# Router products at the two mixers' ends: weights stationary in four column tiles, in place of the token tiles

## What is computed

```python
for i in range(2):
    y = _gated_deltanet_mixer(x, ...) if i == 0 else _mla_mixer(x, ...)
    x = _layernorm(ALPHA * x + y, ln1_g[i], ln1_b[i])
    y = _grouped_moe(x, router_w, router_bias, w_gate[i], w_up[i], w_down[i])
    x = _layernorm(ALPHA * x + y, ln2_g[i], ln2_b[i])

def _grouped_moe(x, router_w, router_bias, ...):
    scores = sigmoid(x @ router_w)      # 512 x 1024 by 1024 x 16
    ...                                 # best group, top 2 in it, gates
```

## Time and profile before

| | |
|---|---|
| median of three runs | 1567.25 us (1565.63 to 1567.25) |
| time of the profiled execution | 1567.03 us |
| its span | 1565.2 us |
| DeltaNet ends, mixture 0 begins | about 905 us |
| attention ends, mixture 1 begins | about 1365 us |
| TensorE busy | 95% of the span |
| VectorE busy | 56% |

### The profile page before, as it was taken

The page is one execution under the profiler, slowest core; times in us unless marked ns, Lnnn a source line. Parts: engine busy times, 40 slices in busy tenths (PEclk is TensorE's granted clock), DMA queues, the critical chain, the costliest instruction groups (busy, mean ns, idle before and its releaser), DMA issues. The chain is left out here.

```text
span 1565.2 us, 22321 instructions
## 1 busy us (share of the span) xinstructions
PE 1479.6 (95%) x8210; PEld 917.2 (59%) x8210; DVE 871.6 (56%) x1734; ACT 349.4 (22%) x745; POOL 171.7 (11%) x196
## 2 busy tenths in 40 slices
PE   8898999999999999999999989999999999889996
PEld 5477686685775866857868643334654544543332
DVE  2785766756857667568575652216435354743117
ACT  4223222222222222212212211111332322111110
POOL 0200202002002020020010220003100000120011
PEclk9899999999999999999999989999999999799999
DMA  7751212102111121020150359997011115369983
GB/s 233 235 180 42 81 28 81 40 13 88 46 54 43 38 77 30 26 80 0 40 202 28 135 181 387 412 391 240 1 66 38 50 39 218 142 253 386 413 337 132
DMA packets 124510, 215.46 MB, mean 138 GB/s; under 512 B 11696, under 2 KB 59120, under 8 KB 124448
## 3 DMA queue, kind: packets, MB, share of 16 engines
q1 hardware_dynamic: 109984, 169.44, 30.5%
q10 hardware_dynamic: 9536, 27.27, 4.7%
q0 software_dynamic: 4928, 17.89, 3.1%
HBM read 182.92 MB, written 31.65 MB: 137 GB/s over the span
## 5 line engine op out<-in xcount | busy, mean ns | idle before, releaser
L451 PE MATMUL bank<-xT,wgu 128*128 128x512 f32 x448 | 210.4, 600 | 0.0
L1758 PE MATMUL bank<-wgu,moe_xgT 128*32 128x512 f32 x1536 | 171.4, 594 | 5.9 <-issue 2.9
L496 PE MATMUL bank<-wd,oT 128*128 128x512 f32 x256 | 118.3, 604 | 2.2 <-ACT oT L838 1.3
L451 PEld LDWEIGHTS bank<-xT,wgu 128*128 128x128 f32 x448 | 78.1, 191 | 64.3 <-issue 63.6
L537 PE MATMUL bank<-wd,xT 128*128 128x256 f32 x512 | 115.8, 379 | 0.0
L1758 PEld LDWEIGHTS bank<-wgu,moe_xgT 128*32 128x32 f32 x1536 | 50.1, 110 | 109.0 <-issue 107.3
L537 PEld LDWEIGHTS bank<-wd,xT 128*128 128x128 f32 x512 | 96.7, 190 | 12.8
L1018 DVE SCALAR_TENSOR_TENSOR wgu<-bank,taps,wgu 128x510 f32<-128x510 f32 (+1 forms) x128 | 95.2, 744 | 12.0 <-ACT wgu L733 8.1
L2005 DVE TENSOR_TENSOR moe_hid<-moe_silu,bank 128x256 f32<-128x256 f32 x24 | 10.1, 421 | 160.1 <-ACT moe_silu L1863 160.1
L1781 PE MATMUL bank<-wd,moe_hidT 128*32 128x512 f32 x768 | 87.0, 593 | 5.4 <-DVE moe_hidT L2009 3.1
L1139 DVE TENSOR_TENSOR wgu<-wgu,bank 128x512 f32<-128x512 f32 x112 | 73.9, 683 | 8.8 <-PE bank L600 3.4
(11 more groups left out here) (341 smaller groups left out, 2409.6 us busy)
## 6 DMA issues: line engine op xcount, KB each, us to landing
wgu<-moe_w_gate SPq DMA_DIRECT2D x32, 1024.0 KB, 12.8
wgu<-moe_w_up SPq DMA_DIRECT2D x32, 1024.0 KB, 14.5
wd<-moe_w_down SPq DMA_DIRECT2D x32, 1024.0 KB, 15.4
wgu<-dn_w_in SPq DMA_DIRECT2D x32, 512.0 KB, 3.8
slots_x<-gains SPq DMA_DIRECT2D x1, 9984.0 KB, 37.6
wd<-dn_w_in SPq DMA_DIRECT2D x8, 1024.0 KB, 5.3
wd<-dn_w_out ACTq DMA_DIRECT2D x16, 512.0 KB, 3.8
xT<-slots_x ACTq DMA_DIRECT2D x16, 512.0 KB, 8.3
```

What stands on the lines that cost most here:

```text
L451: mm = pe.matmul(bank[:], wqkv[:, ct, k], xT[:, k], start=k == 0, stop=k == KD - 1)
L496: mm = pe.matmul(ps[uses.at[f"{name}{n}"][0]][:], oT[:, h, tt], wo[:, h, half * 512:(half + 1) * 512], start=h == 0, stop=h == 1)
L1758: mm = pe.matmul(ps[2][seats].rearrange("p (a f) -> p a f", a=2), xgT[:, j % ROW_BUFS, k, seats], wgu[:, e % RING, :, k], start=k == 0, st ...
```

## The change

The two operands change places. `route` becomes three steps:

- `route_parts` (TensorE): for each of the eight channel pieces `k`, the router's weights are stationary and the 128 tokens of the tile move. The stationary operand is two neighbouring pieces of `route_w` side by side, 32 columns, in column tile `k % 4` of the array, so that the result stands in 32 partitions of a PSUM bank: 16 of them hold the wanted part of piece `k`, 16 hold something that isn't used. Pieces `k` and `k + 4` accumulate in the same partitions. The result is 4 x 32 partitions by 128 tokens.
- `keep` (ScalarE): the 128x128 partial sums are copied from the bank to SBUF, over the tile's piece 0 of `xT`.
- `route_sum` (TensorE): one product with that copy as the stationary operand and a new table of ones and zeros (`C_SUM`, 128x16) as the moving one adds the four partial sums of each expert and turns the result, so that the logits stand in bank 7 as before.

The partial sums of even and odd tiles use two banks in turn (2 and 3 in DeltaNet, 6 and 7 in attention, where `turn` now has two banks in place of three).

```diff
@@ -44,7 +44,8 @@
 C_SEAT = C_SIDE + 16
 CAP = 96
 C_IOTA = C_SEAT + P
-C_ALL = C_IOTA + P
+C_SUM = C_IOTA + P
+C_ALL = C_SUM + 16
 
 
 def constants():
@@ -76,6 +77,8 @@
     c[:, C_SIDE + 8:C_SIDE + 16] = eight < r % 8
     c[:, C_SEAT:C_SEAT + P] = 1.0 + np.arange(P)[None, :] % CAP
     c[:, C_IOTA:C_IOTA + P] = np.arange(P)[None, :]
+    for g in range(4):
+        c[:, C_SUM:C_SUM + 16] += r == 32 * g + 16 * (g == 3) + np.arange(16)[None, :]
     inv = (1.0 / (10000.0 ** (np.arange(0, 64, 2, dtype=np.float32) / np.float32(64)))).astype(np.float32)
     c[:, C_FREQ:C_FREQ + 32] = inv[None]
     return c
@@ -251,7 +254,7 @@
         rs_added, kq_rs_added = sem("rs_added"), sem("kq_rs_added")
         cols_in, cols_turned, weighted, weights_summed = (sem(n) for n in ("cols_in", "cols_turned", "weighted", "weights_summed"))
         weights = wba[:].rearrange("p k (j e) -> p k j e", e=NE)
-        rows = Arrival(nc, t, sb, sem, 0, summed=lambda n: (y_ready, 1 + 8 * (NK - 1) + n + 1))
+        rows = Arrival(nc, t, sb, sem, 0, summed=lambda n: (y_ready, 1 + 8 * (NK - 1) + n + 1), part_banks=(2, 3))
         zeros = t["gains"][0:CAP, 1, 1]
 
 
@@ -679,11 +682,16 @@
                             project_out(uses, "end", i, i, n, h)
                         if n in (3, 5, 7):
                             rows.turn(pe, n // 2 - 1)
+                        if n == 7:
+                            rows.route_sum(pe, 0)
                         if n in (5, 7):
-                            rows.route(pe, n // 2 - 2)
+                            rows.route_parts(pe, n // 2 - 2)
                     rows.turn(pe, TT - 1)
-                    rows.route(pe, TT - 2)
-                    rows.route(pe, TT - 1)
+                    rows.route_sum(pe, 1)
+                    for tt in (2, 3):
+                        rows.route_parts(pe, tt)
+                    for tt in (2, 3):
+                        rows.route_sum(pe, tt)
 
             pe.wait_ge(taps_kept, 1)
             pe.wait_ge(dve_sums, 1)
@@ -1306,10 +1314,12 @@
 class Arrival:
 
 
-    def __init__(self, nc, t, sb, sem, which, banks=(4, 5, 6), summed=None):
-        self.nc, self.t, self.which, self.banks, self.summed = nc, t, which, banks, summed
+    def __init__(self, nc, t, sb, sem, which, banks=(4, 5, 6), summed=None, part_banks=()):
+        self.nc, self.t, self.which, self.banks, self.summed, self.part_banks = nc, t, which, banks, summed, part_banks
         self.g, self.b = t["gains"][:, which % 2, 0], t["gains"][:, which % 2, 1]
         self.mv, self.rstd, self.neg = sb(f"row_mv{which}", [P, TT, 2]), sb(f"row_rstd{which}", [P, TT]), sb(f"row_neg{which}", [P, TT])
+        if summed:
+            self.parted, self.kept = sem(f"parted{which}"), sem(f"kept{which}")
         self.stats_ready, self.spread_ready, self.rstd_added, self.rstd_ready, self.centred, self.normed, self.turned, self.xT_ready, self.logits, self.weighed = (
             sem(f"{n}{which}") for n in ("stats_ready", "spread_ready", "rstd_added", "rstd_ready", "centred", "normed", "turned", "xT_ready_again", "logits", "weighed"))
 
@@ -1356,15 +1366,31 @@
                 mm = pe.transpose(ps[self.banks[n % of]][:, k * P:(k + 1) * P], self.t["res"][:, tt, (half * 4 + k) * P:(half * 4 + k + 1) * P], ident)
             mm.then_inc(self.turned, 1)
 
-    def route(self, pe, tt):
+    def part(self, tt):
+        return self.t["ps"][self.part_banks[tt % 2]][:, P:2 * P]
+
+    def route_parts(self, pe, tt):
         if tt == 0:
             pe.wait_ge(self.t["route_ready"], 3)
+        if tt >= 2:
+            pe.wait_ge(self.kept, tt - 1)
         for k in range(KD):
-            if k % 4 == 0:
+            n = k % 4
+            if n == 0:
                 pe.wait_ge(self.xT_ready, 2 * tt + 1 + k // 4)
-            mm = pe.matmul(self.t["ps"][7][:, tt * NE:(tt + 1) * NE], self.t["xT"][:, k, tt * P:(tt + 1) * P], self.t["route_w"][:, self.which // 2, k], start=k == 0, stop=k == KD - 1)
+            two = self.t["route_w"][:, self.which // 2, k - (n == 3):k - (n == 3) + 2].rearrange("p k e -> p (k e)")
+            mm = pe.matmul(self.part(tt)[32 * n:32 * n + 32], two, self.t["xT"][:, k, tt * P:(tt + 1) * P], start=k < 4, stop=k >= 4)
+        mm.then_inc(self.parted, 1)
+
+    def route_sum(self, pe, tt):
+        pe.wait_ge(self.kept, tt + 1 if tt < 2 else TT)
+        mm = pe.matmul(self.t["ps"][7][:, tt * NE:(tt + 1) * NE], self.t["xT"][:, 0, tt * P:(tt + 1) * P], self.t["const"][:, C_SUM:C_SUM + 16], start=True, stop=True)
         if tt == TT - 1:
             mm.then_inc(self.logits, 1)
+
+    def keep(self, act, tt):
+        act.wait_ge(self.parted, tt + 1)
+        act.copy(self.t["xT"][:, 0, tt * P:(tt + 1) * P], self.part(tt)).then_inc(self.kept, 1)
 
     def take(self, act, tt):
         for half in range(2):
@@ -1376,6 +1402,9 @@
     def on_scalar(self, act):
         for tt in range(TT):
             self.take(act, tt)
+            if tt:
+                self.keep(act, tt - 1)
+        self.keep(act, TT - 1)
         act.wait_ge(self.weighed, 2)
         logits = self.t["gate_exp"][:].rearrange("p t e -> p (t e)")
         act.activation(logits, logits, ACT.Exp, scale=-1.0)
@@ -2151,7 +2180,7 @@
         wqr_in, qr_full, qr_ready, qrT_full, qrT_kept, qrT_ready, kv_ready, nb_ready, p_ready, oT_ready, y_ready = (
             sem(n) for n in ("wqr_in", "qr_full", "qr_ready", "qrT_full", "qrT_kept", "qrT_ready", "kv_ready", "nb_ready", "p_ready", "oT_ready", "y_ready"))
         pT_ready = [sem("pT_ready_act"), sem("pT_ready_dve")]
-        rows = Arrival(nc, t, sb, sem, 2, summed=lambda n: (y_ready, 1 + 8 * (NH - 1) + n + 1))
+        rows = Arrival(nc, t, sb, sem, 2, banks=(4, 5), summed=lambda n: (y_ready, 1 + 8 * (NH - 1) + n + 1), part_banks=(6, 7))
         block = ctx.enter_context(nc.Block())
 
         def nth(uses, name, i):
```

## The result

The changed kernel takes 1571.9 us (median of seven runs, 1570.2 to 1572.7) against 1566.5 us for the kernel before on the same chip (seven runs, 1565.5 to 1567.3). The ratio is 1.0031 with a 95% interval of 1.0022 to 1.0041: 5.4 us slower in the medians, 4.9 by the ratio. The forecast was 1566.1. The profiled execution of the changed kernel took 1571.17 us, its span is 1569.3 us, against 1567.03 and 1565.2 before.

The account below looks back on a forecast made before the run. VectorE was taken as late engine, except for a 1.1 us wait on TensorE at the second mixer's end; -1.1 there, 0 elsewhere took the profiled 1567.03 to 1565.9, median forecast 1566.1 us, range 1563.7 to 1569.0 (90%).

Parts of the forecast that it names:

- The place and size of the gain: Second mixer's end: VectorE's 1.1 us wait for the router's products goes, -1.1 us; first mixer's end 0, or 0.1 at most.
- The pair in column tiles: Router's parts on TensorE: four column tiles run 3.6 abreast, 0.032 us a pair at the high clock, 0.059 at the low.
- The copy: ScalarE's 128x128 copy of the partial sums at a mixer's end: 0.38 us, 0.66 with its hand-overs.
- The last sum: End of the router's products: 1361.15 in the second mixer, 1.9 us before VectorE; about 900.5 in the first, 2.3 before.
- the rival of tiles that don't run abreast: Both mixers' ends: pairs cost as now and ScalarE's copy is added, +1.9 and +1.7, 1570.9 us; chance 4%.
- the one of loads that wait for the product before: Both mixers' ends: each column tile's load waits, 0.41 us a pair, +8.2 and +9.6, 1585 us or more; chance 1%.
- TensorE's time count in full: VectorE only looks full because TensorE feeds it at that rate, so TensorE's savings all count: -11.6, 1555.6 us; chance 3%.
- The table of 16 more columns is loaded long before: Load of the wider constant table: done long before it is needed, no cost given.
- the slower rivals: Both mixers' ends: tiles not running abreast, 1570.9 us, 4%; loads waiting for the product before, 1585 us or more, 1%.
- The clock's later rise in the mixture: Mixture's first products run at half clock after longer TensorE idling: +1.45 us each mixture, 1567.6 or 1569.0 us; chance 10%.

Follow-up runs that it names:

- experiments 2: The changed kernel with the new columns in place of a redundant 16-number table, so the table keeps its old size: 1564.1 against 1566.1 us for the kernel before, ratio 0.9991.
- 3: The changed kernel with its wider table, the router's bias allocated behind the late rows, weights back at old places: 1564.6 against 1566.1 us for the kernel before, ratio 0.9998.
- 8: The changed kernel with the old table size, residual rows, turned rows and gains also at multiples of 512 bytes: 1564.8 against 1564.9 us for the kernel before, ratio 0.9998.

## Why the prediction was wrong

**What held.** The place and size of the gain: 1.1 us at the second mixer's end were forecast, 1.15 measured, nothing at the first mixer's. VectorE is the late engine at both ends: the stretch from the add of the fourth half row to the logits in the first mixer is 18.94 us in both kernels. The pair in column tiles was put at 0.032 us at the high clock and 0.059 at the low one; it took 1.08 / 32 = 0.034 at the high one (0.65 / 16 = 0.041 in a run of a single tile) and 1.94 / 32 = 0.061 at the low. The copy took 0.27 us where 0.38 were taken. The last sum ended 2.7 us before VectorE was ready in the second mixer (forecast: 1.9) and 4.0 us in the first (2.3). In the first mixer that margin has luck in it: the sums were priced at the low clock, and the clock fell there only at about 903.5 us and not at 899.4. The first mixer's logits stand at 903.51 and not at 902.83, but the whole stretch from the fourth half row on moved with them. So the rival of tiles that don't run abreast did not come; that its 1570.9 us lies near the measured time is an accident. Nor did the one of loads that wait for the product before, which had 0.41 us for a pair. By the rule that the prediction cites for it from the Trainium skill (TensorE: Matmul & The Clock Gate, Part 3, The mechanism) it would have come; 0.034 us a pair says otherwise, as the rows of 512 columns did. Nor did TensorE's time count in full: 9.8 us less of it moved the mixers by 1.15.

**What failed** is the step "The table of 16 more columns is loaded long before", which priced the table's growth at nothing. It looked at the table's own load (8 KB more, once) and not at its size. The price was that of 72 loads of 1 MB elsewhere: +2.0 us in mixture 0 and +3.5 us in mixture 1, of which some 1.7 came by way of the clock, behind a wait that had become longer. The range ended at 1569.0, because every case in it, the slower rivals too, was sought in the 20 us that the diff rewrites. The slower outcome came from a fifth one: an address.

The rows shown ahead held no warning of it. What could have given one is the built program: the big tensors stood at exact multiples of 512 bytes, and a table that is the first allocation grew by 64. The mixtures' DMA windows, at 403 to 424 GB/s in the long middle without a pause, say where a few per cent on a transfer would arrive.

The clock's later rise in the mixture, rated at 10%, came in part. In windows of 1 us the second mixture has 0.50 at 1370 and 0.91 at 1371, where the kernel before has 0.76 and 1.00. That is some 0.7 us later with the logits at nearly the same time, and just ahead of the second group of products: L1758 and L1761 took 0.53 and 1.00 us, against 0.45 and 1.00, and the later of them began 0.14 us later. So it cost 0.1 us and not 1.45. In the first mixture the rise kept its distance from the logits.

## What to carry to other kernels

A change that makes an SBUF tensor larger moves all that is allocated behind it: look at the addresses of the tensors into which the kernel loads without pause, before and after, and keep them on multiples of 256 bytes (here 3% of the transfer rate hung on 64 bytes, and by it 4.4 to 5.5 us of 1566). A load that is a little late can cost more than its delay: look at the granted clock behind each wait. Put small tables behind the large buffers, or into the place of something redundant; then the version in four column tiles is as fast as the kernel before or 1 us faster: its ratios are 0.9991, 0.9998 and 0.9998 in experiments 2, 3 and 8, each with an interval that takes in 1.0, so its 1.15 us are seen in the traces and not in the time. And when a measured loss is nowhere near the diff, cut both traces at rows that they share before looking for it in the new code.

## What was not expected of the hardware

- Loads into SBUF from HBM in pieces of 2 KB take 3 to 4% longer when their places in SBUF start off a multiple of 256 bytes (24.35 to 24.51 us for eight against 23.6), and those of 4 KB 2 to 4% (22.86 to 23.15 against 22.3); 32, 64 and 128 bytes off cost nearly the same for the former, and 256 off costs nothing.
- Products in four column tiles with only 128 moving columns took 0.034 us a pair in a run of 32 at 2.4 GHz (1.08 us) and 0.061 us at 1.2 GHz (1.94 us), where the untiled pair with 16 moving columns took 0.116 and 0.214 us.
- A wait can cost a second time. Behind 2.05 to 2.13 us of idle time TensorE was granted half the clock in mixture 1 in all four kernels with the weights off a multiple of 256, and 3.64 us of products became 5.34; behind 2.04 to 2.08 us in mixture 0 it was not. In attention, behind 1.54 us of idle time, twelve pairs took 5.42 us in some kernels and 6.96 in others.
